# Eight modulation tiles moved from the second down stage to the third gate stage, and two norms of one row handled together

## The chip, the cores and the metric

The kernel runs on one core of a Trainium2 chip. A core has a matrix engine (TensorE, "PE"), a vector engine (VectorE, "DVE"), a scalar engine (ScalarE, "ACT"), GpSimd ("POOL") and a queue of DMA instructions on SyncE ("SP"). Each engine works through its own list of instructions in order, and they meet only at semaphores. The metric is the device time in microseconds, the median of several executions; less is better.

## What is computed

A two-layer transformer over 256 tokens (and 16 meta tokens in its first layers) of width 1024 is followed by one block with a context, whose output is normalised again. What matters here are the last norm of the first part, the first norm of the second part, and the modulation:

```python
h = rmsnorm(h, final_norm)                       # ends the first part: "final1"
mod = silu(c) @ w_ada + b_ada                    # 6 x 1024 values: sh1, sc1, g1, sh2, sc2, g2
h1 = rmsnorm(h, norm1_g) * (1 + sc1) + sh1       # "norm1", directly on the result of "final1"
x = x + g1 * gated_merge(...)                    # attention, long convolution, gates
h2 = rmsnorm(x, norm2_g) * (1 + sc2) + sh2
x = x + g2 * ((silu(h2 @ w1) * (h2 @ w3)) @ w2)  # third gate stage, third down stage
out = rmsnorm(x, final_g)                        # "final2"
```

`rmsnorm(x, g)` is `x / sqrt(mean(x*x) + EPS) * g`. The last sixth of the modulation, `g2`, is used only at the very end, in the residual of the third down stage.

## The kernel before

Activations lie transposed: 8 tiles of 128 channels (`h[:, k, :]`), tokens along the free dimension. A product in full precision is three matmuls per 128x128 block of weights, on high and low parts of both sides (`products`, lines 384 to 386). Weights come as chunks of up to 1 MB, alternately into two buffers (`stage[:, b]`). ACT copies a half of a chunk to its high part (`hi_part`, L326), DVE subtracts to get the low part (`lo_part`, L332), and PE waits for the low part. A buffer is loaded again as soon as DVE has made the low parts of what was in it (`load_chunk`, L309, on SP); SP waits for that in the order of its own list.

The stages in order of time are `pool`, `gu0` and `dn0` (gate and down stage of the first feed-forward), `qkv`, `o1`, `gu1`, `dn1`, `k2`, `v2`, `q2`, `hy`, `gates`, attention and convolution, `mix`, `out`, `gu2`, `dn2`. A gate stage has 11 pairs of chunks. In `hidden_stage` DVE does for each chunk: scale the gate's bank to `gate_t` (L1226), a low part of the chunk two further on, scale the other bank to `up_t` (L1230), the second low part, the product of both (L1237 or L1240), and the low part `gl` of the result (L1245). PE may fill a bank again once `up_t` is made. ACT makes a high part, Silu, a high part, `gh` (L828). A down stage has 8 pairs of chunks, one pair for each output tile, and ends each pair with the residual `h` (L1156, L1158).

The modulation is computed on DVE, tile by tile (48 tiles in the order of `ADA_ORDER`): a DMA of 512 KB brings 128 rows of `w_ada` into one of two buffers `adaw[:, b]`, and one DVE instruction multiplies them with `cvec` and sums (`modulate_tile`, L1187; it is followed by two very short ones). The DMA of tile n waits on SP until n-1 tiles are used (`ada`), because the buffer is shared with tile n-2. Of the tiles, 22 are done in `gu0`, 8 in `dn0`, 10 in `gu1` and the last 8, the ones of `g2`, in `dn1`. `adaw`, `cvec` and their scratch share their memory with tensors of the attention and of the gates of the last block.

In `dn1` DVE also prepares the context: `hc` (L1317) is normalised, ACT adds the shift (`modulated`, L919), DVE makes the low part (L1322). Its order of work for one pair is low parts of buffer 0, modulation tile, `hc`, low parts of buffer 1, low part of the context, residual `h`. ACT makes the high parts of buffer 1 after it has added the shift. The order is written out by hand, there is no scheduler.

At the end of `dn1` POOL has summed the squares of the 8 tiles of `h` over the channels of a partition, plainly (`ssq`) and with the squared gain of `final1` (`ssg`); PE sums both over the partitions with a matmul by ones (L436 and L1820), between the first tile and the other three tiles of the keys of the context (`context_keys`). DVE and ACT then compute the inverse root of `final1` (`inverse_root`: L1061, root on ACT, reciprocal L1064), from it the argument of `norm1` (L1451 to L1454), again a root and a reciprocal (L1456), and the product of both (L1457). After that come 8 normalised tiles (L1317) with their high and low parts, which the first tile of `k2` takes one by one.

At the end of `dn2`, POOL squares and adds the eighth tile of `h`, PE sums, and the inverse root of `final2` and eight output tiles follow.

## Time and profile before

| | us |
|---|---|
| median of 3 runs | 1095.29 |
| lowest, highest | 1094.83, 1100.62 |
| the profiled execution | 1099.47 |
| its span, first to last instruction | 1097.7 |
| TensorE's mean granted clock in it | 0.973 of 2.4 GHz |

The profile comes from one execution, the one of 1099.47 us. Its span is 1.77 us shorter than the execution, and the execution is 4.2 us over the median of the three. Start times are counted from the first instruction. A row of the timeline gives start, duration, engine, line, operation, tiles, and in brackets how long the engine had been idle and what ended that. A granted clock of 1.00 is 2.4 GHz, 0.50 is 1.2 GHz.

### The profile page before, as it was taken

The page shows a single profiled execution, that of the slowest core. Times are in us where ns is not written, and L with a number is a line of the kernel's source. Part 1 is how long each engine was busy: PE and PEld are TensorE (multiplying, and loading weights), DVE is VectorE, ACT ScalarE, POOL GpSimd, SP SyncE. Part 2 cuts the span into 40 slices and gives each one's busy share as a digit, 9 for nine tenths or more (in the row PEclk, how much of TensorE's full clock was granted, in tenths as well). Part 3 has the DMA queues.
Part 4 walks back from the last instruction along what each step waited for, and adds up shares of the span by engine and source line. Part 5 has one row for each costly group of instructions (what it writes and reads, how often), then busy time and mean ns, then how long its engine had stood idle before and what let it go on. Part 6 is the DMA issues. An engine that isn't in the chain of part 4 may idle for free.

```text
span 1097.7 us, 20676 instructions
## 1 busy us (share of the span) xinstructions
PE 1029.5 (94%) x7708; PEld 957.4 (87%) x7708; DVE 797.3 (73%) x1304; ACT 494.1 (45%) x746; POOL 177.6 (16%) x179
## 2 busy tenths in 40 slices
PE   6679999999999989999999899999998999999995
PEld 3279999999899879999989787998556999999995
DVE  6979888788766578989678745764665787676554
ACT  3165444344554444455443323566333455554442
POOL 2650000012000056000056202000311060000011
PEclk9789999999999989999999899999899999999998
DMA  6248777566633343666467332453102355544452
GB/s 219 77 153 284 263 256 261 203 232 232 237 116 116 116 171 136 247 231 248 157 229 245 119 116 107 166 188 120 29 25 87 116 193 192 191 178 157 162 185 83
DMA packets 37960, 187.79 MB, mean 171 GB/s; under 512 B 4407, under 2 KB 8280, under 8 KB 24792
## 3 DMA queue, kind: packets, MB, share of 16 engines
q1 hardware_dynamic: 37912, 187.14, 48.2%
q8 instruction: 32, 0.52, 0.2%
q14 instruction: 16, 0.13, 0.0%
HBM read 186.07 MB, written 1.05 MB: 170 GB/s over the span
## 4 chain that ended last, share of the span: by engine, by line
PE 71%; DVE 17%; issue 4%; ACT 4%; DMA 3%; SPq 1%; DVEq 0%; POOL 0%; ACTq 0%; POOLq 0%
PE ps L384 21%; PE ps L386 20%; PE ps L385 20%; DVE wl L332 5%; DVE dump L1187 2%; ACT wh L326 2%; PE ps L1882 1%; PE ps L1895 1%; DMA sini<-in_sini 1%; DMA stage<-in_w_dn 1%; PE ps L1667 1%; DVE xl L1167 1%; PE ps L1861 1%; DMA stage<-in_w_k 1%; PE ps L1906 1%
## 5 line engine op out<-in xcount | busy, mean ns | idle before, releaser
L384 PE MATMUL ps<-xh,wh 128*128 128x256 f32 (+3 forms) x1808 | 524.0, 290 | 17.5 <-DVE xl L1167 8.4
L386 PE MATMUL ps<-xl,wh 128*128 128x256 f32 (+3 forms) x1808 | 521.1, 288 | 0.0
L385 PE MATMUL ps<-xh,wl 128*128 128x256 f32 (+3 forms) x1808 | 520.0, 288 | 0.0
L332 DVE TENSOR_TENSOR wl<-stage,wh 128x1024 fp32r<-128x1024 f32 (+2 forms) x320 | 366.4, 1155 | 126.7 <-ACT wh L326 124.1
L326 ACT ACTIVATE wh<-stage 128x1024 fp32r<-128x1024 f32 (+2 forms) x320 | 306.4, 968 | 209.5 <-PE ps L386 182.7
L384 PEld LDWEIGHTS ps<-xh,wh 128*128 128x128 f32 x1808 | 345.3, 191 | 23.8 <-DVE xl L1167 9.9
L385 PEld LDWEIGHTS ps<-xh,wl 128*128 128x128 f32 x1808 | 345.7, 191 | 1.8 <-issue 0.2
L386 PEld LDWEIGHTS ps<-xl,wh 128*128 128x128 f32 x1808 | 344.1, 190 | 1.4
L384 PE MATMUL ps<-gh,wh 128*128 128x256 f32 (+1 forms) x528 | 150.9, 286 | 6.7 <-DVE wl L332 5.2
L385 PE MATMUL ps<-gh,wl 128*128 128x256 f32 (+1 forms) x528 | 149.4, 283 | 0.0
L386 PE MATMUL ps<-gl,wh 128*128 128x256 f32 (+1 forms) x528 | 149.0, 282 | 0.0
L689 POOL TENSOR_TENSOR norm<-h 128x256 f32 (+1 forms) x40 | 32.8, 819 | 532.7 <-DVE h L1156 297.4
L384 PEld LDWEIGHTS ps<-gh,wh 128*128 128x128 f32 x528 | 99.4, 188 | 8.9 <-DVE wl L332 6.9
L385 PEld LDWEIGHTS ps<-gh,wl 128*128 128x128 f32 x528 | 99.2, 188 | 0.0
L386 PEld LDWEIGHTS ps<-gl,wh 128*128 128x128 f32 x528 | 99.2, 188 | 0.0
L828 ACT ACTIVATE gh<-up_t 128x256 f32 (+3 forms) x66 | 27.9, 423 | 116.1 <-DVE up_t L1240 77.4
L1187 DVE CUSTOM_DVE_ANT_0 dump<-adaw,cvec 128x1024 bf16<-128x1024 f32 x40 | 52.5, 1313 | 0.0
L823 ACT ACTIVATE gate_t<-gate_t 128x256 f32<-128x256 f32 (+1 forms) x66 | 29.9, 452 | 31.5 <-DVE gate_t L1226 31.3
L1245 DVE TENSOR_TENSOR gl<-up_t,gh 128x256 f32 (+3 forms) x66 | 28.5, 432 | 17.8 <-ACT gh L828 17.3
L691 POOL TENSOR_TENSOR norm<-norm 128x256 f32<-128x256 f32 (+1 forms) x40 | 36.3, 906 | 3.1
L1230 DVE TENSOR_TENSOR up_t<-ps,norm 128x272 f32<-128x272 f32 (+2 forms) x66 | 28.1, 426 | 4.3 <-PE ps L386 4.1
L1226 DVE TENSOR_TENSOR gate_t<-ps,norm 128x272 f32<-128x272 f32 (+2 forms) x66 | 28.1, 426 | 1.0 <-PE ps L386 0.7
(237 smaller groups left out, 873.4 us busy)
## 6 DMA issues: line engine op xcount, KB each, us to landing
stage<-in_w_gu SPq DMA_DIRECT2D x66, 1024.0 KB, 4.8
stage<-in_w_dn SPq DMA_DIRECT2D x48, 704.0 KB, 4.1
adaw<-in_w_ada SPq DMA_DIRECT2D x48, 512.0 KB, 5.0
stage<-in_w_gates SPq DMA_DIRECT2D x8, 1024.0 KB, 4.8
stage<-in_w_hy SPq DMA_DIRECT2D x6, 1024.0 KB, 4.8
stage<-in_w_q SPq DMA_DIRECT2D x8, 512.0 KB, 5.1
stage<-in_w_k SPq DMA_DIRECT2D x8, 512.0 KB, 4.9
stage<-in_w_v SPq DMA_DIRECT2D x8, 512.0 KB, 5.1
```

The lines of the kernel that those rows point to most:

```text
L326: nc.scalar.activation(wh[:, b, w], stage[:, b, w], ACT.Copy).then_inc(split_hi, 1)
L332: nc.vector.tensor_tensor(wl[:, b, w], stage[:, b, w], wh[:, b, w].bitcast(fp32), ALU.subtract).then_inc(split_lo, 1)
L384: nc.tensor.matmul(psum, wh[:, b, w], xhi, start=first and n == 0, stop=False)
L385: nc.tensor.matmul(psum, wl[:, b, w], xhi, start=False, stop=False)
L386: last = nc.tensor.matmul(psum, wh[:, b, w], xlo, start=False, stop=close and n == len(blocks) - 1)
L689: pool.tensor_tensor(sq[:, 0:width], hk, hk, ALU.mult).then_inc(squared, 1)
L691: pool.tensor_tensor(ssq[:, 0:width], ssq[:, 0:width], sq[:, 0:width], ALU.add)\
L823: act.activation(gate_t[:, b, 0:width], gate_t[:, b, 0:width], ACT.Silu, **({"bias": gate_t[:, b, width:width + 1]} if shifted else {}))\
L1187: ins = dve.tensor_tensor_reduce(out=dump[:, 0, :], in0=adaw[:, b, :], in1=cvec[:, 0, :], scale=1.0, scalar=0.0, op0=ALU.mult, op1=ALU.add ...
L1226: dve.tensor_tensor(gate_t[:, b, 0:w], ps[2 * b][:, 0:w], rstd[:, 0:w], ALU.mult)\
L1230: dve.tensor_tensor(up_t[:, b, 0:w], ps[2 * b + 1][:, 0:w], rstd[:, 0:w], ALU.mult)\
L1245: dve.tensor_tensor(gl[:, ds(m, 1), 0:width], up_t[:, b:b + 1, 0:width], gh[:, ds(m, 1), 0:width].bitcast(fp32), ALU.subtract).then_inc(ac ...
```

## The change

Three parts. (1) The eight tiles of `g2` leave `dn1`. They are computed in pairs 1 to 4 of `gu2`, one in each chunk. SP loads `cvec` again after the first pair of chunks of `gu2`, since its memory has been used for other things in between, ACT applies Silu to it again, and four trips of a loop on SP each issue two tiles of `w_ada` and then one pair of chunks of `gu2`. (2) For `norm1` the two means give the argument of one root directly, mean(gained)/D + EPS*(mean/D + EPS); the root of `final1` itself is computed after the tiles of `norm1`. (3) The squares of the last tile are made on ACT, with and without the gain, into `gate_t`, and PE adds them by a second matmul to each sum; the same, plainly, for `final2`, before which ACT loads its table for the root at the start of `dn2`.

```diff
--- before.py
+++ after.py
@@ -71,8 +71,9 @@
              + [(4, k) for k in range(6, 8)] + [(5, k) for k in range(8)])
 
 STAT = {n: i + 1 for i, n in enumerate(("pool", "ffn0", "attn", "ffn1", "ctx", "final1", "norm1", "norm2", "final2"))}
-ROOT = {n: i + 1 for i, n in enumerate(("pool", "ffn0", "attn", "ffn1", "ctx", "final1", "norm1", "norm2", "final2"))}
+ROOT = {n: i + 1 for i, n in enumerate(("pool", "ffn0", "attn", "ffn1", "ctx", "norm1", "final1", "norm2", "final2"))}
 RES0 = {n: KD * i for i, n in enumerate(("pool", "dn0", "o1", "dn1", "out", "dn2"))}
+SUM0 = {"pool": 0, "dn0": 8, "o1": 16, "dn1": 24, "out": 31, "dn2": 39}
 IN0 = {n: KD * i for i, n in enumerate(("pool", "dn0", "o1", "ctx", "x2", "out"))}
 
 G1, SH2, SC2A, SH1, SC1, SC2B, G2 = 0, 8, 16, 22, 30, 38, 40
...
@@ -432,9 +434,16 @@
 
         def norm_sum(n, width):
 
-            nc.tensor.wait_ge(summed, KD + RES0[n])
+            nc.tensor.wait_ge(summed, KD + SUM0[n])
             nc.tensor.matmul(ps[6][:, 0:width], ones[:, :], ssq[:, 0:width], start=True, stop=True)\
                 .then_inc(stats, 1)
+
+        def norm_sum_in_parts(n, bank, sums, gained, last):
+
+            nc.tensor.wait_ge(summed_gained if gained else summed, KD - 1 + (0 if gained else SUM0[n]))
+            nc.tensor.matmul(ps[bank][:, 0:TX], ones[:, :], sums, start=True, stop=False)
+            nc.tensor.wait_ge(last_squared, {"dn1": 1, "dn2": 3}[n] + gained)
+            nc.tensor.matmul(ps[bank][:, 0:TX], ones[:, :], last, start=False, stop=True).then_inc(stats, 1)
 
         block = ctx.enter_context(nc.Block())
@@ -611,12 +620,12 @@
                 ada(SC2B + b, b)
             for b in range(2):
                 load_chunk("gu1", PAIR0["gu1"] + 10, b)
-            dn("dn1", G2, before=())
+            chunks("dn1")
 
             load_chunk("k2", PAIR0["k2"], 0)
             load_chunk("k2", PAIR0["k2"], 1)
             sp.wait_ge(used, 4 * PAIR0["k2"])
-            sp.wait_ge(ada_used, 48)
+            sp.wait_ge(ada_used, G2)
             sp.dma_start(rope[:, :, :], A["rope"].rearrange("p (a b) -> p a b", a=2)).then_inc(mixer_const_in, 16)
             sp.dma_start(swap[:, :], A["swap"]).then_inc(mixer_const_in, 16)
             for u in range(2):
@@ -632,8 +641,24 @@
                     sp.dma_start(bias[:, u, :], A["bias"][ds((2 * g + u) * P, P), :]).then_inc(bias_in[u], 16)
             for b in range(2):
                 load_chunk("mix", PAIR0["mix"] + 1, b)
-            for s in ("out", "gu2", "dn2"):
-                chunks(s)
+            chunks("out")
+            for b in range(2):
+                load_chunk("gu2", PAIR0["gu2"], b)
+            sp.wait_ge(inv, 6)
+            sp.dma_start(cvec[:, 0, :], A["cc"][0:1, :].rearrange("a b -> (a b)").partition_broadcast(P))\
+                .then_inc(cvec_in, 16)
+            for b in range(2):
+                load_chunk("gu2", PAIR0["gu2"] + 1, b)
+            sp.wait_ge(na_scored, 2 * NA_HEADS)
+            with sp.Fori(0, 4) as g:
+                for b in range(2):
+                    ada(2 * g + (G2 + b), b)
+                for b in range(2):
+                    load_chunk("gu2", g + (PAIR0["gu2"] + 2), b)
+            with sp.Fori(6, NCHUNK["gu2"] // 2) as g:
+                for b in range(2):
+                    load_chunk("gu2", g + PAIR0["gu2"], b)
+            chunks("dn2")
 
             for k in range(KD):
                 sp.wait_ge(fin_ready, k + 1)
...
@@ -930,10 +955,14 @@
             through(act, "dn1", dn1_chunk, hi_part, unroll=2)
 
-            root("final1", TX)
+            act.wait_ge(res, KD + RES0["dn1"])
+            act.activation(gate_t[:, 0, 0:TX], h[:, KD - 1, 0:TX], ACT.Square).then_inc(last_squared, 1)
+            act.activation(gate_t[:, 1, 0:TX], h[:, KD - 1, 0:TX], ACT.Square, scale=col("final1", KD - 1))\
+                .then_inc(last_squared, 1)
             root("norm1", TX, rstd1)
             for k in range(KD):
                 modulated("x2", nt, 0, k, mods[:, SH1 + k:SH1 + k + 1])
+            root("final1", TX)
 
             for s in ("k2", "v2", "q2"):
                 through(act, s, splits_only, hi_part)
@@ -1042,8 +1071,13 @@
             through(act, "out", o_hi_next("out", "norm2", TX), hi_part)
             late_splits("out", hi_part)
             root("norm2", TX)
+            act.wait_ge(cvec_in, 32)
+            act.activation(cvec[:, 0, :], cvec[:, 0, :], ACT.Silu).then_inc(cvec_ready, 1)
             hidden_stage(2, TX, shifted=True)
+            act.preload_act_table(ACT.Sqrt)
             through(act, "dn2", splits_only, hi_part, unroll=2)
+            act.wait_ge(res, KD + RES0["dn2"])
+            act.activation(gate_t[:, 0, 0:TX], h[:, KD - 1, 0:TX], ACT.Square).then_inc(last_squared, 1)
             root("final2", TX)
 
         @block.vector
@@ -1250,7 +1284,7 @@
 
                 def one_tile(pair, b):
 
-                    n0 = (0, SC2B - 16)[f]
+                    n0 = (0, SC2B - 16, G2 - 2)[f]
                     return lambda: modulate_tile(n0 + 2 * pair + b, pair + n0 // 2, b)
                 last = KF // 2 - 1
                 plain = 0
@@ -1264,6 +1298,13 @@
                                   lambda: modulate_second(2 * t + (SC1 + u), u))
                     for b in range(2):
                         chunk(8, b, within(8, b), one_tile(8, b))
+                if f == 2:
+                    plain = 5
+                    for b in range(2):
+                        chunk(0, b, within(0, b))
+                    with dve.Fori(1, plain) as g:
+                        for b in range(2):
+                            chunk(g, b, within(g, b), one_tile(g, b))
                 with dve.Fori(plain, last) as g:
                     for b in range(2):
                         chunk(g, b, within(g, b), None if f else one_tile(g, b))
@@ -1442,24 +1483,23 @@
                                               op0=ALU.add, op1=ALU.mult))
             link(dve.tensor_tensor(gain1[:, 5, :], gain1[:, 0, :], col("final1", 0, 8), ALU.mult))
             inverse_root("ctx", TX, 6)
-            down_stage("dn1", TX, None, G2, context=True)
-
-
-
-            inverse_root("final1", TX, 6)
+            down_stage("dn1", TX, context=True)
+
+
+
+            dve.wait_ge(stats, STAT["final1"])
+            link(dve.tensor_scalar(stat[:, 0:TX], ps[6][:, 0:TX], EPS / D, EPS * EPS, ALU.mult, ALU.add))
             dve.wait_ge(stats, STAT["norm1"])
-            link(dve.scalar_tensor_tensor(out=stat[:, 0:TX], in0=ps[7][:, 0:TX], scalar=1.0 / D, in1=rstd[:, 0:TX],
-                                          op0=ALU.mult, op1=ALU.mult))
-            link(dve.tensor_tensor(stat[:, 0:TX], stat[:, 0:TX], rstd[:, 0:TX], ALU.mult))
-            dve.tensor_scalar(stat[:, 0:TX], stat[:, 0:TX], EPS, None, ALU.add).then_inc(mean_ready, 1)
+            dve.scalar_tensor_tensor(out=stat[:, 0:TX], in0=ps[7][:, 0:TX], scalar=1.0 / D, in1=stat[:, 0:TX],
+                                     op0=ALU.mult, op1=ALU.add).then_inc(mean_ready, 1)
             dve.wait_ge(root_ready, ROOT["norm1"])
             link(dve.reciprocal(rstd1[:, 0:TX], rstd1[:, 0:TX]))
-            link(dve.tensor_tensor(rstd1[:, 0:TX], rstd1[:, 0:TX], rstd[:, 0:TX], ALU.mult))
             for k in range(KD + 1):
                 if k < KD:
                     normed("x2", nt, h, gain1[:, 5, k:k + 1], rstd1, k)
                 if k:
                     normed_lo("x2", nt, 0, k - 1, mods[:, SH1 + k - 1:SH1 + k])
+            inverse_root("final1", TX, 6)
 
             def copies(s, dst, width, scale=None):
                 def chunk(pair, b, u, ahead):
@@ -1623,7 +1659,10 @@
             dve.wait_ge(prod_re, 4)
             inverse_root("norm2", TX, 6)
             link(dve.memset(rstd[:, TX:TX + 1], 1.0))
+            dve.wait_ge(cvec_ready, 2)
             hidden_stage(2, TX, shifted=True)
+            dve.wait_ge(mods_ready, 48)
+            link(dve.tensor_tensor(mods[:, G2:48], mods[:, G2:48], col("b_ada", G2, 8), ALU.add))
             down_stage("dn2", TX, None, None, None, lambda m: mods[:, ds(G2 + m, 1)])
             inverse_root("final2", TX)
             for k in range(KD):
@@ -1815,9 +1854,8 @@
             pe.wait_ge(nlo, KD + IN0["ctx"])
             context_keys(0, 0)
             pe.wait_ge(mean_ready, ROOT["ctx"])
-            norm_sum("dn1", TX)
-            pe.wait_ge(summed_gained, KD)
-            pe.matmul(ps[7][:, 0:TX], ones[:, :], ssg[:, :], start=True, stop=True).then_inc(stats, 1)
+            norm_sum_in_parts("dn1", 6, ssq[:, 0:TX], 0, gate_t[:, 0, 0:TX])
+            norm_sum_in_parts("dn1", 7, ssg[:, :], 1, gate_t[:, 1, 0:TX])
             context_keys(0, 1)
             context_keys(1, 0)
             context_keys(1, 1)
@@ -1969,7 +2007,7 @@
             two_tiles("gu2", wide(0, TX + 2), TX + 2, (res, (RES0["out"] + 6, RES0["out"] + 8)), (nlo, IN0["out"] + 1),
                       lambda: norm_sum("out", TX))
             down("dn2", 2, TX)
-            norm_sum("dn2", TX)
+            norm_sum_in_parts("dn2", 6, ssq[:, 0:TX], 0, gate_t[:, 0, 0:TX])
 
 # ---- launch: the host lays data out; arrays of constants depend on shapes alone
```

The queue of SP from the last chunks of `out` on, before (`stage<-in_w_gu` is a chunk of `gu2`, in a loop over its pairs):

```order
L309 DMA stage<-in_w_out 128x2048
L536 REGISTER_ALU
L536 COMPARE_AND_BRANCH
L536 UNCONDITIONAL_BRANCH
L536 ISA
L309 ISA [waits weights_lo]
L309 DMA stage<-in_w_gu 128x2048
```

and in the changed kernel, where L653 is the loop of four trips, after two pairs of chunks that stand singly:

```order
L311 DMA stage<-in_w_gu 128x2048 [waits weights_lo] x2
L648 DMA cvec<-in_cc 128x1024 [waits inverse]
L311 DMA stage<-in_w_gu 128x2048 [waits weights_lo] x2
L653 UNCONDITIONAL_BRANCH [waits na_scored]
L653 ISA
L552 ISA [waits ada_used]
L552 DMA adaw<-in_w_ada 128x1024
L552 ISA [waits ada_used]
L552 DMA adaw<-in_w_ada 128x1024
L310 ISA
L311 ISA [waits weights_lo]
L311 DMA stage<-in_w_gu 128x2048
```

Two waits for used tiles now stand ahead of the loads of each of the pairs 2 to 5. ACT at the start of `gu2`, between the high parts of the first chunk and the loop, before:

```order
L764 ACT_TABLE_LOAD
L764 ACTIVATE norm<-norm 128x256
L830 ACT_TABLE_LOAD
L352 UNCONDITIONAL_BRANCH
L352 ISA
L325 ISA
L326 ACTIVATE wh<-stage 128x1024
```

and changed:

```order
L789 ACT_TABLE_LOAD
L789 ACTIVATE norm<-norm 128x256
L1075 ACT_TABLE_LOAD
L1075 ACTIVATE cvec<-cvec 128x1024
L855 ACT_TABLE_LOAD
L354 UNCONDITIONAL_BRANCH
L354 ISA
L327 ISA
L328 ACTIVATE wh<-stage 128x1024
```

One more table load and the Silu of `cvec` now stand ahead of the first high part.

## Rows read from the trace of the kernel before

**Rows 1.** Page, part 1: busy time, share of the span, instructions

```profile
PE 1029.5 (94%) x7708; PEld 957.4 (87%) x7708; DVE 797.3 (73%) x1304; ACT 494.1 (45%) x746; POOL 177.6 (16%) x179
```

**Rows 2.** Windows, `dn1`: stretch, length, busy time by engine, PEclk, DMA share, GB/s

```profile
534.00:604.30 70.30, 65.05 (x533) 63.21 (x532) 54.72 (x90) 27.28 (x43) 32.89 (x28) 1.00 0.64 224
```

**Rows 3.** Timeline, DVE, one pair of `dn1`

```profile
587.15 1.76 DVE L1187 CUSTOM_DVE_ANT_0 dump<-adaw,cvec 128x1024 bf16<-128x1024 f32 x1
...
589.38 0.48 DVE L1317 SCALAR_TENSOR_TENSOR hc<-hc,gain,norm 128x256 f32 x1 [0.19 <-issue]
591.39 1.69 DVE L332 TENSOR_TENSOR wl<-stage,wh 128x768 fp32r<-128x768 f32 x2 [1.52 <-ACT wh L326]
...
593.40 0.41 DVE L1156 TENSOR_TENSOR h<-ps,h 128x256 f32 x1
```

**Rows 4.** Timeline, PE: starts after idle time in `dn1`, after it, and in `dn2`

```profile
544.30 0.40 PE L384 MATMUL ps<-gh,wh 128*128 128x256 f32 x1 [1.47 <-DVE wl L332]
...
592.40 0.39 PE L384 MATMUL ps<-gh,wh 128*128 128x256 f32 x1 [0.57 <-DVE wl L332]
...
608.66 0.55 PE L384 MATMUL ps<-xh,wh 128*128 128x256 f32 x1 [4.05 <-DVE xl L1322]
...
1027.25 0.39 PE L384 MATMUL ps<-gh,wh 128*128 128x256 f32 x1 [0.48 <-DVE gl L1245]
```

**Rows 5.** Windows, columns as in rows 2: first context tile

```profile
608.66:613.90 5.24, 5.24 (x24) 5.24 (x25) 2.92 (x3) 0.00 (x0) 4.66 (x4) 0.50 0.78 266
```

**Rows 6.** Timeline, DVE, from the sums to the first tile of `norm1`

```profile
614.68 0.42 DVE L1061 TENSOR_SCALAR norm<-ps 128x256 f32<-128x256 f32 x1 [3.10 <-PE ps L436]
...
619.08 1.75 DVE L1456 RECIPROCAL norm<-norm 128x256 f32<-128x256 f32 x1 [0.48 <-ACT norm L764]
...
621.32 0.88 DVE L1317 SCALAR_TENSOR_TENSOR hyu<-h,gain,norm 128x256 f32<-128x256 f32 x2
```

**Rows 7.** Timeline, PE: sums, next context tile, last product of `k2`'s first tile

```profile
613.92 0.73 PE L436 MATMUL ps<-norm,ones 128*128 128x256 f32 x2
...
614.73 0.47 PE L384 MATMUL ps<-xh,wh 128*128 128x256 f32 x1
...
628.34 0.39 PE L384 MATMUL ps<-xh,wh 128*128 128x256 f32 x1
```

**Rows 8.** Timeline, DVE and PE, the end of the program

```profile
1085.80 0.48 DVE L1158 SCALAR_TENSOR_TENSOR h<-ps,mods,h 128x256 f32<-128x256 f32 x1 [5.78 <-PE ps L386]
...
1087.94 0.70 PE L436 MATMUL ps<-norm,ones 128*128 128x256 f32 x2 [2.18 <-POOL norm L691]
```

**Rows 9.** Timeline, ACT and DVE, the start of `gu2`

```profile
902.08 1.28 ACT L830 ACT_TABLE_LOAD   x1
903.38 1.06 ACT L326 ACTIVATE wh<-stage 128x1024 fp32r<-128x1024 f32 x1
...
913.53 0.43 DVE L1226 TENSOR_TENSOR gate_t<-ps,norm 128x257 f32<-128x257 f32 x1
```

**Rows 10.** Timeline, DVE, one chunk of `gu0` with its modulation tile

```profile
85.05 0.43 DVE L1226 TENSOR_TENSOR gate_t<-ps,norm 128x272 f32<-128x272 f32 x1
...
88.43 1.22 DVE L1187 CUSTOM_DVE_ANT_0 dump<-adaw,cvec 128x1024 bf16<-128x1024 f32 x1
...
90.39 0.44 DVE L1226 TENSOR_TENSOR gate_t<-ps,norm 128x272 f32<-128x272 f32 x1
```

**Rows 11.** Page, part 6, and the tile `adaw` at 72 us: times to landing

```profile
stage<-in_w_gu SPq DMA_DIRECT2D x66, 1024.0 KB, 4.8
...
L577 SPq DMA_DIRECT2D adaw<-in_w_ada x2: 433/433/433, 72.3 to 72.7; - x2
...
DMA to landing us min/median/max: 5.7/6.1/6.5
```

**Rows 12.** Timeline, ACT in `gu2`: high parts that wait for PE

```profile
941.72 1.06 ACT L326 ACTIVATE wh<-stage 128x1024 fp32r<-128x1024 f32 x1 [1.07 <-PE ps L386]
...
947.52 1.06 ACT L326 ACTIVATE wh<-stage 128x1024 fp32r<-128x1024 f32 x1 [1.00 <-PE ps L386]
```

More of the change, by code:

```diff
@@ L268, in build @@
         summed_gained = sem("summed_gained")
+        last_squared = sem("last_squared")
         nhi = sem("input_hi")
@@ L681, in _, with squares @@
                 .then_inc(late_ready, 1)
-            def squares(n, width):
+            def squares(n, width, count=KD):
                 link(pool.memset(ssq[:, 0:width], 0.0))
-                with pool.Fori(0, KD) as k:
+                with pool.Fori(0, count) as k:
                     pool.wait_ge(res, k + 1 + RES0[n])
@@ L689, in squares @@
                     pool.tensor_tensor(sq[:, 0:width], hk, hk, ALU.mult).then_inc(squared, 1)
-                    pool.wait_ge(squared, k + 1 + RES0[n])
+                    pool.wait_ge(squared, k + 1 + SUM0[n])
                     pool.tensor_tensor(ssq[:, 0:width], ssq[:, 0:width], sq[:, 0:width], ALU.add)\
                         .then_inc(summed, 1)
-                    pool.wait_ge(summed, k + 1 + RES0[n])
+                    pool.wait_ge(summed, k + 1 + SUM0[n])
             def squares_gained(n):
@@ L698, in squares_gained @@
                 link(pool.memset(ssg[:, :], 0.0))
-                for k in range(KD):
+                for k in range(KD - 1):
                     pool.wait_ge(res, k + 1 + RES0[n])
@@ L703, in squares_gained @@
                     pool.tensor_tensor(sq[:, 0:TX], h[:, k, 0:TX], h[:, k, 0:TX], ALU.mult).then_inc(squared, 1)
-                    pool.wait_ge(squared, k + 1 + RES0[n])
+                    pool.wait_ge(squared, k + 1 + SUM0[n])
                     pool.tensor_tensor(ssq[:, 0:TX], ssq[:, 0:TX], sq[:, 0:TX], ALU.add).then_inc(summed, 1)
-                    pool.wait_ge(summed, k + 1 + RES0[n])
+                    pool.wait_ge(summed, k + 1 + SUM0[n])
                     link(pool.tensor_scalar(sq[:, 0:TX], sq[:, 0:TX], gain1[:, 4, k:k + 1], None, ALU.mult))
@@ L750, in _ @@
             pool.wait_ge(stats, STAT["norm2"])
-            squares("dn2", TX)
+            squares("dn2", TX, KD - 1)
         @block.scalar
@@ L1504, in _ @@
             through(dve, "hy", conv_sides, lo_part)
-            dve.wait_ge(mods_ready, 48)
-            link(dve.tensor_tensor(mods[:, G2:48], mods[:, G2:48], col("b_ada", G2, 8), ALU.add))
             for k in range(KD):
```

## The prediction

> **What bounds the kernel now.** I read the busy shares first: TensorE is busy for 94% of the span [rows 1]. Where it runs without a pause, nothing done beside it counts, and a change pays only where it waits. So the next view is its idle time and what ended it. It waits in `dn1` (65 us busy of 70 [rows 2]), each time for a low part [rows 4]; for 4.05 us before the first context tile, for `xl` [rows 4]; and at the end, for POOL's squares [rows 8]. In `gu2` it never waits: there ACT waits for it, at 941.72 and 947.52, each time for the end of a chunk [rows 12]. A chunk is thus 5.80 us and a pair 11.6 us; counted on from the second chunk, which begins at 900.9, and with 0.27 us for the hand-over, pair 4 begins at 941.45 and pair 3 at 929.85.
>
> **dn1 without its tiles.** One pair on DVE [rows 3]: the tile with its two short followers takes 587.15 to 589.38 (2.2 us), then `hc`, ACT's shift and high part (1.52 us of waiting), two low parts, the residual. Nothing here waits for TensorE; TensorE waits for this chain. It does pair 1 to 7 from 544.30 to 604.35 (608.66 less 4.05 of idle time and the 0.28 us of its last product), 8.58 us a pair. The same work unhindered is `dn2`: from 1027.25, the middle of pair 0, to the residual at 1085.80 [rows 4, 8] are 7.5 pairs, 7.79 us each. Without the tile the chain is 8.58 - 2.2 = 6.4 us, below 7.79, so TensorE becomes the bound: 7 x (8.58 - 7.79) = **5.5 us** gained. The low bound counts only the idle times on the rows, some 0.4 to 1.0 us a pair, 4.0 us in all. The first wait (1.47 us, for the root of the context) stays.
>
> **The pause behind dn1.** Today it is 4.3 us from the end of `dn1` to 608.66. In the new order the last `hc` comes right behind the residual of pair 6, and what is left behind it is the shift (0.5), one high part (1.05, from when pair 7's first buffer is free, 3.9 us before the end), two low parts (2.9) and `xl` (0.4). By that chain `xl` is ready 0.9 us after TensorE's end: **3.4 us** gained. With so short a pause I expect the clock to stay up, as it did through all the pauses of up to 1.5 us in `dn1` (1.00 in rows 2). Today the first context tile runs at a granted clock of 0.50 for 5.24 us [rows 5]; at full clock it is half a chunk, 2.85 us: **2.4 us** gained, none if the clock falls all the same.
>
> **The sums and the norm.** Two sums of one matmul each take 0.81 us today (613.92 to 614.73 [rows 7]); two more cost **0.8 us**. The second pair needs ACT's squares, which follow the two high parts of `k2`'s second chunk: 0.25 + 2 x 1.05 + 2 x 0.42 = 3.0 us after the end of `dn1`, before the sums at 0.9 + 2.85 = 3.75: hidden. POOL's seventh tile is done by the end of `dn1`, hidden too. From the sums to the first tile of `norm1` are 6.64 us today (614.68 to 621.32 [rows 6]); then eight tiles of 0.79 us each feed `k2`'s first tile, which ends at 628.7, where the context tiles end at 623.1 (614.73 and three tiles of 2.8) [rows 7]. The new chain is one argument (0.45), root (0.5) and reciprocal (1.75): 2.7 us. The eighth tile is ready 2.7 + 6.9 = 9.6 us after the sums, when TensorE, after 8.4 us of context tiles, is at its fourth block of 24 products: no wait. `k2`'s first tile takes 2.85 instead of 5.6 us: **2.75 us** gained. The root of `final1` moved behind it takes 2.7 us on DVE, with 8.5 us of `k2` products as its cover.
>
> **The end.** POOL's two instructions (0.68 and 0.78 us with their hand-overs, 1086.47 to 1087.94) give way to one of 0.42 us on ACT, and the second sum follows: 1086.3 + 0.5 + 0.4 against 1088.65 today; **1.15 us** gained.
>
> Gains: 5.5 + 3.4 + 2.4 - 0.8 + 2.75 + 1.15 = **14.4 us**; low end 14.4 - 1.5 - 2.4 = 10.5.
>
> **gu2 with the tiles.** DVE has room for a tile: a chunk of `gu0` with one takes 90.39 - 85.05 = 5.34 us [rows 10], about 5.4 here, under 5.80. What has no room is SP. In each trip of its new loop it waits until both tiles of the pair before have been used, and only then issues the next pair of chunks. The tile of a chunk is done late: 88.43 + 1.22 - 85.05, 4.65 us after the chunk's gate is read. So buffer 0 of pair 3, today issued in chunk (1,0), is issued at the end of (1,1), when DVE and ACT want it next. I follow it:
> - Start: a second table load (1.28) and the Silu of `cvec` (1.05) stand before the first high part at 903.38 [rows 9]: everything behind is 2.3 us later. Chunk (1,0) begins at 913.53 + 2.3 = 915.84 [rows 9], (1,1) at 921.24; its tile is done at 925.9. (This start alone would hold TensorE for 1.9 us; the later waits swallow that.)
> - Landing: 1 MB takes 4.8 us [rows 11]. Of two transfers of 512 KB issued 0.4 us apart, median 6.1 and longest 6.5 say that they landed after 5.7 and 6.5, the second 1.25 us behind the first. So 1 MB streams for 2.5 us, the fixed part is 2.3, and a chunk issued right behind a tile lands 0.1 + 2.3 + 1.25 + 2.5 = 6.15 us after the release: 932.05.
> - From landing to TensorE: high part 1.1, low part 1.2, `up_t` 0.45, semaphore 0.1: 2.85 us. Pair 3 starts at 934.9, 5.05 us behind 929.85.
> - The cycle: from one landing to the gate of the chunk after it 6.15 us (high, Silu, high, low, product, tile, `gl`), 4.65 to the end of its tile, 6.15 to the next landing: 16.95 us against TensorE's 11.6. It comes twice more (pairs 4 and 5): 2 x 5.35 = 10.7 us.
> - From pair 6 on the loads are free again. Behind the last wait, of 3 to 5.7 us, the clock should be low as it was behind 4.05 us [rows 5]: 2.4 us more. Behind the other two waits this is swallowed by the next.
> Cost: 5.05 + 10.7 + 2.4 = **18.15 us**. Bounds: 13.35 if the chunk lands 4.8 us after its issue in spite of the tile before it (three times 0.8) and the clock stays up; 26 if the two chunks of a trip share the engines and land together (three times 2.5).
>
> The moved sum of `b_ada` (0.2 us), the wait before it and the table load at the start of `dn2` (1.28 us, against 3.9 us of products in pair 0's second half) are hidden; today's load before `final2` was hidden as well.
>
> On the table loads the row decides: the high part starts 0.02 us after the load ends [rows 9]. The Trainium skill, in "ScalarE: Activation LUTs", section "What ACT_TABLE_LOAD costs", adds a drain of about 1.38 us to every switch; by that the start, and with it every landing, would be 1.4 us later, a rival of its own below.
>
> **Sum.** 18.15 - 14.4 = +3.75 us on the profiled span: 1097.7 becomes 1101.5. The profiled execution was 4.2 us over the median; nothing shows that the change touches that, so I add the difference to the median: **1099.0 us**.
>
> **Rivals.**
> - A, the loads are in time after all: the release comes early enough and only the start costs, 1.9 us. 1095.3 - 14.4 + 1.9 = 1082.8. Against it: buffer 0 is wanted 0.7 us after its issue. 0.08.
> - B, half of it: DVE catches up more than I think, so that TensorE's slack of 8.5 us between reading a gate and needing the next pair takes up one of three waits (5.4) and the clock stays up (2.4). 1091.2. 0.10.
> - C, slower: the two chunks of a trip share the DMA engines, so the first lands up to 2.5 us later each time; 3 x 2.5 = 7.5: 1106.5. It decides once the first chunk lands more than 7 us after its release. The order of landing [rows 11] speaks against it, but with 512 KB pieces. 0.14.
> - D, the gains come short: the clock falls in the pause behind `dn1` all the same, and `dn1` gives 4.0: 1099.0 + 3.9 = 1102.9. 0.13.
> - E, every table switch drains: the start is 1.4 us later, 1100.4. 0.02.
> - Forecast, 1096 to 1102: 0.53.
>
> A measurement of this kernel can tell about 0.5% (5.5 us) from no change. Faster by more: A, and 0.05 of B, 0.13. Slower by more: C, 0.10 of D and 0.06 of the forecast's upper edge, 0.30. Within: 0.57. The range leaves out A and the upper half of C: 1088 to 1107.
>
> **What would show it.** In the new profile: `dn1` 7.8 us a pair with no waits for `wl` but the first; a pause under 1.5 us before the context tiles and a clock of 1.00 in them; 2.7 us from the sums to the first tile of `norm1`; in `gu2` three waits of TensorE for low parts of pairs 3, 4 and 5, with pairs some 17 us apart; the chunk's DMA issued behind that of a tile. No such waits would make the forecast wrong by up to 16 us.

## The result and the profile after

The changed kernel takes 1103.51 us (median of 13 runs, 1098.58 to 1106.40) where the kernel before takes 1095.26 (13 runs, 1094.53 to 1100.62): ratio 1.0061, 95% interval 1.0044 to 1.0078. It is slower by about half a per cent. The profiled execution took 1103.91 us with a span of 1102.1, against 1099.47 and 1097.7: 4.4 us more.

Page, part 1, of the changed kernel, to be held against [rows 1]. TensorE is as busy as before in microseconds (1029.3 against 1029.5) at nearly the same mean clock (0.972 against 0.973), so the 4.4 us more of span are idle time:

```profile
PE 1029.3 (93%) x7714; PEld 959.5 (87%) x7714; DVE 792.7 (72%) x1302; ACT 497.1 (45%) x751; POOL 165.5 (15%) x173
```

**dn1 and what follows it.** Timeline of PE (start, duration, engine, line, operation, tiles, idle time before and its releaser), and the stretches of `dn1` and of the first context tile (length, busy time of PE, weight loads, DVE, ACT, POOL, granted clock, DMA share, GB/s), as [rows 2, 4, 5, 7]:

```profile
544.12 0.39 PE L386 MATMUL ps<-gh,wh 128*128 128x256 f32 x1 [1.47 <-DVE wl L334]
...
599.47 0.36 PE L386 MATMUL ps<-xh,wh 128*128 128x256 f32 x1 [0.71 <-issue]
...
602.38 0.59 PE L444 MATMUL ps<-norm,ones 128*128 128x256 f32 x2
...
603.92 0.47 PE L386 MATMUL ps<-xh,wh 128*128 128x256 f32 x1
```

```profile
534.00:598.76 64.76, 63.29 (x532) 62.65 (x530) 45.63 (x68) 29.86 (x44) 29.44 (x30) 1.00 0.54 183
599.47:602.38 2.91, 2.91 (x24) 2.91 (x25) 2.59 (x3) 2.10 (x4) 0.00 (x0) 1.00 0.80 214
```

Only the first wait for `wl` is left, the pause is 0.71 us, and the context tile runs at 1.00 (2.4 GHz). DVE between the sums and the first tile of `norm1`, against [rows 6]:

```profile
603.44 0.42 DVE L1491 TENSOR_SCALAR norm<-ps 128x256 f32<-128x256 f32 x1 [1.14 <-PE ps L446]
604.38 0.42 DVE L1493 SCALAR_TENSOR_TENSOR norm<-ps,norm 128x256 f32<-128x256 f32 x1 [0.52 <-PE ps L446]
605.29 1.75 DVE L1496 RECIPROCAL norm<-norm 128x256 f32<-128x256 f32 x1 [0.48 <-ACT norm L789]
607.08 0.88 DVE L1358 SCALAR_TENSOR_TENSOR hyu<-h,gain,norm 128x256 f32<-128x256 f32 x2
```

From the argument of the root to the first tile it is 2.70 us.

**gu2.** Timeline of PE: every start after more than 0.45 us of idle time from the end of `out` to the middle of the first pair of `dn2`, and the end of the program (against [rows 4, 8]):

```profile
894.52 0.38 PE L386 MATMUL ps<-xh,wh 128*128 128x258 f32 x1 [1.66 <-DVE up_t L1264]
...
921.44 0.58 PE L386 MATMUL ps<-xh,wh 128*128 128x258 f32 x1 [3.46 <-DVE up_t L1264]
...
938.47 0.58 PE L386 MATMUL ps<-xh,wh 128*128 128x258 f32 x1 [3.86 <-DVE up_t L1264]
...
955.87 0.58 PE L386 MATMUL ps<-xh,wh 128*128 128x258 f32 x1 [4.21 <-DVE up_t L1264]
...
1032.78 0.38 PE L386 MATMUL ps<-gh,wh 128*128 128x256 f32 x1 [0.47 <-DVE gl L1279]
...
1092.33 0.70 PE L446 MATMUL ps<-gate_t,ones 128*128 128x256 f32 x2 [0.59 <-ACT gate_t L1080]
```

The queue of SyncE, then ACT, then DVE around the first of the three waits (the two tiles of a trip are one row with x2, and so are its two chunks):

```profile
907.39 5.71 SPq L552 DMA_DIRECT2D adaw<-in_w_ada  x2
913.43 0.87 SPq L311 DMA_DIRECT2D stage<-in_w_gu  x2
```

```profile
918.65 1.06 ACT L328 ACTIVATE wh<-stage 128x1024 fp32r<-128x1024 f32 x1 [6.64 <-DMA stage<-in_w_gu]
```

```profile
911.37 1.22 DVE L1221 CUSTOM_DVE_ANT_0 dump<-adaw,cvec 128x1024 bf16<-128x1024 f32 x1
912.51 0.08 DVE L1221 DVE_READ_ACCUMULATOR2_ANT moda<- 128x1 f32 x1
...
919.74 1.23 DVE L334 TENSOR_TENSOR wl<-stage,wh 128x1024 fp32r<-128x1024 f32 x1 [5.98 <-ACT wh L328]
```

So reads a wait behind a wait: the tile of chunk (1,1) is done at 912.59, the next tile is issued for it, the chunk at 913.43 behind that, its high part starts at 918.65, and TensorE at 921.44. ACT, DVE and TensorE all stand idle in between, TensorE last in the row and for the shortest time. SyncE's waits from 895 to 960 (engine, line, what it waited for, us, times, longest) say who held the queue:

```profile
SPq L552 <- DVE moda L1221: 39.8, 6, 9.6
SPq L311 <- DVE wl L334: 20.4, 3, 8.5
```

### The profile page after: what moved, and what is told of

Same layout as the page of the kernel before. It is cut to its first block, busy times and chain, and to the rows that moved or that the text cites. A ratio compares the mean times of both kernels' runs of the same rounds, so it can differ in the third digit from the quotient of the medians.

```text
span 1102.1 us, 20702 instructions
## 1 busy us (share of the span) xinstructions
PE 1029.3 (93%) x7714; PEld 959.5 (87%) x7714; DVE 792.7 (72%) x1302; ACT 497.1 (45%) x751; POOL 165.5 (15%) x173
## 4 chain that ended last, share of the span: by engine, by line
PE 72%; DVE 14%; DMA 4%; ACT 4%; issue 4%; SPq 1%; DVEq 0%; ACTq 0%; POOL 0%
PE ps L386 21%; PE ps L388 21%; PE ps L387 21%; DVE wl L334 4%; DMA stage<-in_w_gu 2%; ACT wh L328 2%; DVE dump L1221 1%; PE ps L1920 1%; PE ps L1933 1%; DMA sini<-in_sini 1%; PE ps L1706 1%; DVE xl L1201 1%; PE ps L1899 1%; DMA stage<-in_w_k 1%; PE ps L1944 1%
## 5 line engine op out<-in xcount | busy, mean ns | idle before, releaser
L386 PE MATMUL ps<-xh,wh 128*128 128x256 f32 (+3 forms) x1808 | 525.3, 291 | 26.4 <-DVE up_t L1264 13.8
L1221 DVE CUSTOM_DVE_ANT_0 dump<-adaw,cvec 128x1024 bf16<-128x1024 f32 x40 | 49.3, 1232 | 0.0
```

Source lines behind the costliest of these rows:

```text
L386: nc.tensor.matmul(psum, wh[:, b, w], xhi, start=first and n == 0, stop=False)
L1221: ins = dve.tensor_tensor_reduce(out=dump[:, 0, :], in0=adaw[:, b, :], in1=cvec[:, 0, :], scale=1.0, scalar=0.0, op0=ALU.mult, op1=ALU.add ...
```

## Experiments

Each was compared with the kernel before on its own chip: e1 to e4 on one (before 1096.95 us), r5, e6, e7 and e8 on a second (1098.01), e9, e10 and r11 on a third (1099.03), e12 on a fourth (1097.03). Theory Q: the loads come late because they stand in SyncE's queue behind the waits for used tiles. Its rivals: the work of the tiles itself, or the bytes (V); the table switch.

**e1: each chunk ahead of its tile.**

```diff
 with sp.Fori(0, 4) as g:
     for b in range(2):
-        ada(2 * g + (G2 + b), b)
-    for b in range(2):
         load_chunk("gu2", g + (PAIR0["gu2"] + 2), b)
+        ada(2 * g + (G2 + b), b)
```

> The changed kernel with one edit: in SyncE's loop of four trips each chunk of gu2 is issued ahead of the modulation tile of its buffer (chunk, tile, chunk, tile, as in gu0), instead of both tiles first. Theory Q (SyncE's queue holds the chunks back): the three waits of TensorE at pairs 3, 4 and 5 (3.5, 3.9 and 4.2 us in the changed kernel's trace) and the slow clock behind them go, only the start's 1.7 us stays: about 17.5 us less than the changed kernel, near 1086, and faster than the kernel before by 0.8%. Rival V (a tile in each chunk is too much for VectorE, or 512 KB more per chunk too much for the DMA engines): the waits stay or spread over more pairs, and the time stays within 4 us of the changed kernel's 1103.5.

Measured 1085.24 us (5 runs), ratio 0.9895 (0.9874 to 0.9917), near the 1086 expected. In `gu2` one wait of PE is left, that of the start; SyncE issues the chunk of each buffer 1.5 us before its tile:

```profile
888.26 0.38 PE L386 MATMUL ps<-xh,wh 128*128 128x258 f32 x1 [1.66 <-DVE up_t L1263]
```

```profile
910.50 0.33 SPq L311 DMA_DIRECT2D stage<-in_w_gu  x1
912.03 0.33 SPq L552 DMA_DIRECT2D adaw<-in_w_ada  x1
915.87 0.33 SPq L311 DMA_DIRECT2D stage<-in_w_gu  x1
```

Same instructions, same bytes, another order in one queue: between the ratios of the changed kernel and of e1 lie 1.66%, 18 us, where 16.25 were forecast (18.15 less the 1.9 of the start). In the traces the stretch from `mix` to the middle of `dn2`'s first pair takes 197.66 us in the changed kernel, 180.02 in e1 and 178.11 in the kernel before: the queue cost 17.6 us, and the start 1.9. Q stands; V falls.

**e2: e1 without the second table load at the start of `gu2`.**

```diff
-                act.preload_act_table(ACT.Silu)
+                if f < 2:
+                    act.preload_act_table(ACT.Silu)
```

> As e1_loads_ahead, and ACT's second table load at the start of gu2 (behind the Silu of cvec, whose table is the same) is left out. If a switch costs what the row shows (1.28 us), TensorE's wait at pair 1 shrinks from 1.7 to about 0.4 us and the time is 1.3 us under e1_loads_ahead. If a drain comes with every load, 2.7 us can't all show, since the wait is only 1.7 us: then it vanishes altogether.

Measured 1080.57 us (5 runs), ratio 0.9864 (0.9840 to 0.9888). The wait of 1.66 us shrinks to 0.24:

```profile
888.42 0.38 PE L386 MATMUL ps<-xh,wh 128*128 128x258 f32 x1 [0.24 <-DVE up_t L1264]
```

By the expectation, about 0.4 us left speaks for the price of the row, and no wait at all would have spoken for a drain. ACT at the start of `gu2` in e1, and in e2:

```profile
881.36 0.42 ACT L788 ACTIVATE norm<-norm 128x256 f32<-128x256 f32 x1 [2.54 <-DVE norm L1094]
881.80 1.28 ACT L1074 ACT_TABLE_LOAD   x1
883.09 1.06 ACT L1074 ACTIVATE cvec<-cvec 128x1024 f32<-128x1024 f32 x1
884.17 1.28 ACT L854 ACT_TABLE_LOAD   x1
```

```profile
883.38 1.28 ACT L1075 ACT_TABLE_LOAD   x1
884.68 1.06 ACT L1075 ACTIVATE cvec<-cvec 128x1024 f32<-128x1024 f32 x1
885.64 1.04 ACT L328 ACTIVATE wh<-stage 128x1024 fp32r<-128x1024 f32 x1
```

From the end of the root to the high part there are 3.7 us in e1 and 2.3 in e2, 1.4 less: the load of 1.28 us, and 0.1 us by which the high part now overlaps the Silu. The intervals of the two ratios overlap, so these 1.4 us are seen in the trace only (the medians differ by 4.7). In the rows of e1 each instruction behind a load begins 0.01 us after its end.

**e3: parts 2 and 3 alone, the tiles stay in `dn1`; e4: all three parts, but no tiles of `g2` at all** (the eight tiles are left out with their loads, the second `cvec` and its Silu; `g2` is `b_ada` alone). The diff shows the main lines of each.

```diff
 e3, on SP and DVE; the loop of gu2 is a plain chunks("gu2")
-            chunks("dn1")
+            dn("dn1", G2, before=())
-            down_stage("dn1", TX, context=True)
+            down_stage("dn1", TX, None, G2, context=True)
 e4
-            link(dve.tensor_tensor(mods[:, G2:48], mods[:, G2:48], col("b_ada", G2, 8), ALU.add))
+            link(dve.tensor_copy(mods[:, G2:48], col("b_ada", G2, 8)))
```

> Parts 2 and 3 of the change alone: the eight tiles stay in dn1, gu2 is as before; one root for norm1, the last tile's squares on ACT. By the prediction's terms: sums 0.8 us dearer, k2's first tile 2.75 us shorter, the end 1.15 us shorter: 3.1 us under the kernel before, 1092.2; the waits in dn1, the pause of 4.3 us behind it and the slow clock of the first context tile stay. Rival: POOL's squares, not DVE's chain, held the sums back, so that the shift of one tile to ACT brings them forward too and more than 4 us are gained.

> The changed kernel without the eight tiles: no DMA of them, no second cvec, no products; g2 is then b_ada alone, so that part of the computation is left out. It is the floor of what moving the tiles can reach. Theory Q: gu2 runs without a wait, 19.6 us under the changed kernel: near 1084, and 1.5 to 2 us under e1_loads_ahead. Theory V: well below e1_loads_ahead, by 10 us or more.

e3: 1091.88 us (12 runs), ratio 0.9963 (0.9942 to 0.9984), which is 1.8 to 6.4 us where 3.1 were expected; the waits of `dn1` and the pause of 4.05 us are as before. In place it is 1.9 us from the first context tile to the first wait in `q2` (61.15 against 63.04) and 1.16 at the end (59.53 against 60.69), 3.05 us together: the expectation holds, and the rival, that POOL held the sums back, falls. e4: 1083.36 (6 runs), ratio 0.9869 (0.9843 to 0.9895). 1.31% of 1096.95 is 14.4 us (interval 11.5 to 17.2), the sum of the predicted gains. e2 with the tiles is within the interval of e4 without: rightly queued, eight tiles in `gu2` cost nothing that the times can tell, and 0.75 us in the trace (178.86 us from `mix` to the middle of `dn2`'s first pair against 178.11).

**r5: the kernel before again; e6: the changed kernel, and e9: the kernel before, with filled pauses.** The runs of one kernel spread over 4 to 10 us, and their mean clock goes with it (r5: 0.976 to 0.978 at 1095.3 to 1098.1, 0.973 at 1099.7 to 1101.0). In the attention of the last block TensorE pauses three times for 2.2 us. Theory P: what the clock does behind these pauses makes the spread, and the changed kernel's excess over the forecast.

```diff
 in na_turn(u)
+                if u in (3, 10, 12):
+                    pe.wait_ge(na_prt, u - 1)
+                    for i in range(12):
+                        pe.transpose(ps[2 + b][:, i % 4 * P:(i % 4 + 1) * P], ident[:, :], ident[:, :])
                 pe.wait_ge(na_prob, u + 1)
```

> The kernel before, unchanged, to see its own spread. In the profiles so far TensorE pauses three times for 2.2 us in the attention of the last block, and the stretch from the first score after the pause of 0.94 us (763.47) to the first product of `mix` (849.14) took 85.67 us in the kernel before and in the changed one, 84.03 in e4, and 80.8 in e1, e2 and e3. Theory P (the clock after these pauses differs from run to run and makes nearly all of the spread): a run with mean clock 0.973 takes about 1099.5, one with 0.976 about 1097, one with 0.978 about 1095; here the stretch is 80.8 us if the profiled run is under 1096, about 85.7 if it is over 1099. Theory N (the spread comes from elsewhere): the stretch doesn't follow the run's time.

> The changed kernel with 12 transposes of the identity in front of the 4th, 11th and 13th turn of the attention, into the bank that the turn then overwrites, where TensorE pauses for 2.2 us. Theory P (the clock after these pauses is why the changed kernel came out 4 us over the forecast): the clock stays at 1.00 in the attention, the stretch takes 80.8 to 81.3 us, the median is 1098.5 to 1100 and all runs lie within 3 us. Theory N (the extra is in the clock behind the waits of gu2 or elsewhere): the stretch is short too, but the median stays at 1102 or above with a spread of 6 us or more.

> The kernel before with the three pauses of the attention filled by transposes, as in e6. In the profiles the filled stretch takes 79.2 us against 84.0 to 85.7 unfilled in the kernel before, and the runs of the kernel before spread over 6 to 7 us. Theory P (the clock after these pauses makes the spread of the kernel before): all runs within 3 us, the median 1.5 us under the lowest unfilled run of the same chip, since the lowest has the clock up (80.8) and filling gives another 1.6. Theory N: the spread stays over 5 us and the median falls by less than 3 us. If the changed kernel suffers more from these pauses than the one before (theory S), the median falls here by less than the 6 us that filling took from the changed kernel; if both suffer alike, by as much.

The clock behind the first of these pauses in the changed kernel (769.97) and, from the same place on, in e1 (768.58), by windows of one length; e1 does 38 matmuls in it, the changed kernel 20:

```profile
769.97:777.73 7.76, 7.76 (x20) 4.35 (x21) 2.54 (x11) 2.59 (x9) 0.00 (x0) 0.56 0.11 34
```

```profile
768.58:776.34 7.76, 7.76 (x38) 5.06 (x39) 4.92 (x19) 3.76 (x12) 0.00 (x0) 1.00 0.14 36
```

The pause is 2.20 us both times, the clock behind it 0.56 or 1.00. Read off the starts of PE, from the first score to `mix` it is 85.67 us in both first profiles, 84.05 in r5, 82.45 in r11, 84.03 in e4, 80.8 in e1 to e3 and 79.2 in e6 to e9 and e12: from each pause to the next 3.3, 1.6 or 0 us were lost against the filled kernels. The kernel before again (r5) took 1098.38 us (12 runs), ratio 0.9996 (0.9980 to 1.0012). Filled, the kernel before takes 1091.53 us (6 runs), ratio 0.9935 (0.9919 to 0.9951), and the changed one 1097.65 (12 runs), ratio 0.9999 (0.9983 to 1.0015). Both gain 6 to 7 us. So these pauses are dear, but they cost the two kernels alike: P is wrong as to the excess. The quotient of the two ratios, 1.0064, is that of the unfilled kernels. As to the spread it is wrong for these two as well, where other long pauses are left: 4.6 us (e9) where the kernel before had 4.8 on that chip, and 5.2 us (e6). And r5, whose profiled execution took 1099.16 us, lost 4.85 us there and not the 6.5 that I had expected of such a run. What else makes the spread stays open.

**r11: the changed kernel again.**

> The changed kernel, unchanged, on the same chip as e9, with the clock of each run. On the first chip it was 1103.5 against 1095.3; the profiles, both with a stretch of 85.67 us in the attention, differ by 4.4. Theory S: the ratio to the kernel before is again 1.004 to 1.008 and the runs lie mostly at a clock of 0.972. Theory T (the rest of the difference was the luck of one chip): the ratio is 1.002 to 1.004.

1103.84 us (6 runs), ratio 1.0053 (1.0037 to 1.0068); by medians 4.8 us, not 8.25. That is S, and T falls: the changed kernel is slower by half a per cent here too. Its trace shows that one term of the queue's cost varies. PE at pair 4, SyncE's issue of pair 4's chunks, and the high part of the first of them:

```profile
936.60 0.58 PE L386 MATMUL ps<-xh,wh 128*128 128x258 f32 x1 [6.78 <-DVE up_t L1264]
```

```profile
926.70 0.87 SPq L311 DMA_DIRECT2D stage<-in_w_gu  x2
```

```profile
933.80 1.06 ACT L328 ACTIVATE wh<-stage 128x1024 fp32r<-128x1024 f32 x1 [8.53 <-DMA stage<-in_w_gu]
```

Here the chunk took 7.10 us from its issue to the high part. Over three traces of this queue the nine first chunks took 5.22, 5.49, 5.86 (changed kernel), 5.77, 7.10, 5.51 (r11), 7.49, 7.07 and 5.46 us (e6).

**e12: does the second chunk take DMA engines from the first?** On e6:

```diff
-                for b in range(2):
-                    load_chunk("gu2", g + (PAIR0["gu2"] + 2), b)
+                load_chunk("gu2", g + (PAIR0["gu2"] + 2), 0)
+                sp.wait_ge(landed[0], 16 * (g + (PAIR0["gu2"] + 3 - QKV_PAIRS)))
+                load_chunk("gu2", g + (PAIR0["gu2"] + 2), 1)
```

> e6 (the changed kernel with the attention's pauses filled), and in the loop of four trips SyncE issues the second chunk of a pair only when the first has landed. In three profiles of the changed queue the first chunk of pairs 3, 4 and 5 reached ACT's high part 5.22, 5.49, 5.86, then 5.77, 7.10, 5.51, then 7.49, 7.07 and 5.46 us after its issue, and gu2 (from the first product of `mix` to the middle of dn2's pair 0) took 197.66, 197.5 and 199.38 us. Theory C (the second chunk, issued 0.5 us behind, takes engines from the first in some trips): all three are 4.8 to 5.4 us here, the cycles 16.4 to 17.0 us, and though the second chunk is then 0.3 to 1 us late the stretch is 197 to 198.5 and the spread of the runs is smaller than the 5.2 us of e6. Theory M (the landing varies for another reason): some of the three take over 6 us all the same.

The three took 5.67, 6.48 and 5.76 us, the stretch 196.2; 1097.00 us (12 runs, 1093.14 to 1103.17), ratio 0.9997 (0.9980 to 1.0014), the same as e6. One landing over 6 us with nothing but tiles ahead of it speaks for M, and the spread did not shrink (10.0 us, on another chip than e6's 5.2); that none is over 7 may be chance. The second chunks, now alone in the queue, were in use 4.84, 4.84 and 4.82 us after their issue.

The DMA view shows how the late trips differ. GB/s in r11 in 40 slices of 0.15 us, from 932 to 938, around the end of the late trip (chunk issued at 926.70, in use 7.10 us later), and from 950 to 956, around that of the next trip (issued at 945.34, in use 5.51 us later):

```profile
GB/s 382 437 437 273 546 273 492 382 492 382 437 219 0 109 0 109 0 55 0 55 0 55 0 55 0 0 0 0 0 0 0 0 0 0 0 0 0 0 0 0
GB/s 382 492 382 492 382 492 328 546 328 546 328 492 328 546 273 219 55 55 0 0 0 0 0 0 0 0 0 0 0 0 0 0 0 0 0 0 0 0 437 0
```

In the late trip nearly all bytes of both chunks have come by 933.8, and then single portions trickle in until 935.5, at 55 GB/s in every other slice. That is some 27 GB/s, by an estimate about the share of one of the 16 engines in the 400 before. The same tail stands behind the other two trips over 7 us (e6, to 916.3 and 934.9), and a shorter one behind e12's 6.48; in the quick trips it is 0.7 us or less. In all nine trips of the three kernels the first chunk is in use 1.7 to 1.9 us before the last byte of the second has come. So a late chunk is not short of bandwidth; a small part of it comes late, and that happens with the second chunk held back too. Why it does stays open.

**e7: e2 with filled pauses; e8: e7 without part 3; e10: e7 without part 2.** The diff of e7 is those of e2 and e6 together; e8 and e10 put the lines of the kernel before back into e7.

> e2 (each chunk of gu2 issued ahead of its tile, one table load less) with the same filled pauses. Theory P: e2's runs lay at 1079.2 to 1080.6 with a mean clock of 0.983, and at 1083.8 to 1085.4 with 0.977; with the pauses filled all runs lie at 1079 to 1081. Theory N: the median stays near 1081 to 1083 with runs up to 1085.

> e7 with part 3 undone: POOL squares and adds the last tile in dn1 and dn2 as in the kernel before, and each sum is one matmul. My theory: the end is 1.15 us longer, and behind dn1 the two missing matmuls give 1.1 us back (the four of the changed kernel took 602.38 to 604.26, against 0.81 us for two before), so e8 is within 0.5 us of e7. Rival: POOL's four instructions for the last tile, some 2.7 us with the gain, are late for the sums behind dn1, which come 3 us after the last product of dn1; then e8 is 1.5 to 2.5 us slower than e7.

> e7 with part 2 undone: the root of final1, then the argument of norm1 from it, then the second root, as in the kernel before. By the prediction's step: the chain from the sums to the first tile of norm1 takes 6.6 us instead of 2.7, and the first tile of k2 takes 5.6 us instead of 2.85, so the kernel is 2.75 us slower than e7 (about 1082.7 where e7 is 1080.0). Rival: the chain ends 3.9 us later and all of it shows, 3.9 us; or TensorE has slack left that the step didn't count, under 1.5 us.

e7: 1080.00 us, five runs from 1079.29 to 1080.50, ratio 0.9833 (0.9810 to 0.9855). No pause over 1.5 us is left behind the start of `dn1`, and the spread is 1.2 us over five runs, against 6.2 in e2: here P's forecast holds. (e8, which has two pauses more, of 1.8 and 2.2 us, spreads over 4.7 us, and e10 over 2.2.) It is the best version, 1.7% under the kernel before.

e8: 1082.67 us (6 runs), ratio 0.9859 (0.9836 to 0.9881), 2.7 us over e7 by medians. My theory falls, the rival stands. PE in e8 behind `dn1`, and POOL ahead of it:

```profile
604.26 0.70 PE L1853 MATMUL ps<-ssg,ones 128*128 128x256 f32 x2 [1.81 <-POOL ssg L732]
```

```profile
599.24 0.61 POOL L727 TENSOR_TENSOR norm<-h 128x256 f32<-128x256 f32 x1 [1.89 <-DVE h L1184]
599.93 1.60 POOL L729 TENSOR_TENSOR norm<-norm 128x256 f32<-128x256 f32 x1
601.63 1.77 POOL L731 TENSOR_SCALAR norm<-norm,gain 128x256 f32<-128x256 f32 x1
603.49 0.72 POOL L732 TENSOR_TENSOR ssg<-ssg,norm 128x256 f32<-128x256 f32 x1
```

POOL takes 5.0 us for the last tile, where I had counted 2.7. The trace of the kernel before had it at this very place, from 608.98 to 614.01, up to the sums:

```profile
608.98 1.52 POOL L703 TENSOR_TENSOR norm<-h 128x256 f32<-128x256 f32 x1 [1.89 <-DVE h L1156]
...
613.28 0.73 POOL L708 TENSOR_TENSOR ssg<-ssg,norm 128x256 f32<-128x256 f32 x1
```

There the pause of 4.05 us hid it; once part 1 has closed the pause, part 3 is what keeps TensorE from waiting. From the context tile to the first wait in `q2` it is 61.70 us in e8 and 58.98 in e7, and the end is 1.15 us longer (59.55 and 60.70 from the middle of `dn2`'s first pair to the last sum). That makes 3.9 us in place, where the spans differ by 2.7; 0.8 of the rest lies between `q2` and the attention, where the edit does nothing (see the gains below).

e10: 1081.88 us (5 runs), ratio 0.9848 (0.9831 to 0.9866), 1.9 us over e7 by medians, 1.6 by the ratios, whose intervals overlap; in place 61.01 us against 58.98, so part 2 gives 2.0 us, where 2.75 were expected and the rivals had 3.9 or under 1.5. (e10's profile has 1.7 us more in the attention, see below.)

## Point by point

- **dn1, 5.5 us**: pairs 1 to 7 took 54.64 us (544.12 to 598.76) against 60.05: 5.4. Right.
- **The pause, 3.4, and its clock, 2.4**: 4.31 became 0.71 us (3.6), and the tile behind it took 2.91 instead of 5.25 (2.3). Right.
- **Sums, -0.8**: 1.54 us (602.38 to 603.92) against 0.81. Right. That POOL's last tile would have cost TensorE 1.8 us of waiting in the new place was not seen, for the prediction priced part 3 against the old pause; it did no harm, since all parts came together.
- **`k2`'s first tile, 2.75**: from the second context tile to the first wait in `q2` 54.49 us against 56.97: 2.5, and 2.0 by e10. Right, a little high; why is not shown.
- **The end, 1.15**: residual to sum 0.98 us against 2.14: 1.16. The number is right, its working is not: 1086.3 + 0.5 + 0.4 against 1088.65 is 1.45. It comes to 1.15 with the 0.7 us that the row of the sums shows [rows 8].
- **Gains, 14.4**: up to the attention 13.8 us and at the end 1.16, together 15.0. But 0.7 of it lies from `q2` to the attention, where the change does nothing: that stretch takes 91.0 or 91.8 us from run to run, in the kernel before (91.8, in e9 91.0) as in the changed one (91.0, in e6 91.8). Without it the gains are 14.3; e4 gives 14.4 by its ratio. Right.
- **The queue, 5.05 + 10.7 + 2.4 = 18.15**: TensorE reached pair 3 5.6 us late, the next two cycles took 17.03 and 17.40 us against 16.95 forecast and 11.6 unhindered (11.2 more), and the remainder of `gu2` 2.7 us more, by the low clock:

```profile
955.87:960.00 4.13, 4.13 (x19) 4.13 (x20) 3.95 (x8) 1.84 (x4) 0.00 (x0) 0.50 0.43 129
```

  Together 19.5. At the first wait it was 2.79 us from landing to TensorE (2.85 forecast) and 6.06 from release to landing (6.15). The mechanism is right in each link. (The 4.65 us to the end of the tile are 4.60 by the rows they are taken from, which changes nothing.) The size was too low: from `mix` to the middle of `dn2`'s first pair it is 197.66 us in the changed kernel, 197.5 in r11 and 199.4 in e6, against 178.1 in the kernel before and e9 (177.7 in r5), so the cost is 19.4 to 21.3. The term that was mis-sized is the landing: 6.15 us from the release was near the quickest case, and three of nine chunks took 7 us and more even from their issue, 7.9 to 8.3 from the release. That is the sign that the prediction had named for rival C, and C had priced it as three times 2.5 us; it came in one trip of three, by some 1.7 us over the others, and e12 and the tails in the DMA view speak against C's cause, the second chunk. The start was priced at 1.9 us; PE's wait there is 1.66, and e1's stretch is 1.9 longer.
- **The table**: ACT's row shows the high part 0.02 us behind the load, in the changed kernel as before. The drain that the Trainium skill names for every switch to a different set, in "ScalarE: Activation LUTs", section "What ACT_TABLE_LOAD costs", does not show here: in e1 the root ends at 881.78, the load of Silu's table runs from 881.80 to 883.08, and the Silu starts at 883.09. Rival E falls.
- **From span to median, the step that failed.** On the profile +3.75 was forecast and +4.4 measured. That this is so near is in part luck: the cost was 1.4 us higher than forecast, and the 0.7 us between `q2` and the attention fell to the changed kernel's side. Then I took off the 4.2 us by which the profiled execution lay over the median of three, "nothing shows that the change touches that". The profile of the changed kernel lay 0.4 us over its median, and there went 3.8 of the 4.5 us between 1099.0 and 1103.51. Both profiles had lost 6.5 us behind the pauses of the attention. That the runs of the kernel before near 1095 had lost less there is likely, but no trace of one of them shows it. On the other chips the median of the kernel before was 1097.0 to 1099.0, and that of the changed kernel 4.8 us above it on the one of them where both ran. The difference of two spans with the same losses was a better estimate than any absolute time.

The range and the sign held: slower by 0.5 to 0.6%, on the upper side of the forecast and at the edge of what I had called the same.

## What to carry to other kernels

Before work is moved next to a stream of loads, write down the queue that issues both: a wait for a consumer that stands ahead of another buffer's load costs a whole round of release, landing and conversion (17 us a pair here where TensorE needs 11.6), while the same instructions interleaved the other way cost 1.9 us, all of it at the start, and 0.75 with one table load less. Price each part against the kernel that the other parts leave: POOL's squares were hidden by a pause that part 1 removed. Take a duration from the place in question where the trace has it: POOL's 5.0 us stood there. And compare profile with profile stage by stage before you believe a median's absolute value.
